# Scores of two B steps on four row groups, V products of A and C two steps together, and key and value up-projections moved into the first steps

## The chip, the cores and the metric

The kernel runs on one core of a Trainium2 chip. The core has five engines that work side by side, each through its own list of instructions in order: PE (TensorE, matrix products, with the loading of its stationary operand shown apart as PEld), DVE (VectorE), ACT (ScalarE), POOL (GpSimd) and SP (SyncE, which here only starts transfers). They meet at semaphores. The metric is the time of the program on the device in microseconds (us), the median of several executions.

## The reference

```python
# D_MODEL 1024, SEQ 512, DEPTH 2; each layer mixes four groups of 256 columns, then projects out
A = _mla(cq, ckv, krope, ...)          # q, k_nope and v come from small up-projections w_uq, w_ukv
B = _diff_attn(q, k, v, ...)           # 4 heads x 2 maps of depth 32; softmax of each, then a1 - lam * a2
C = _dsa(q, k, v, qidx, kidx, ...)     # attention over the topk keys that an index picks
D = _short_conv(b, c, h, conv_w)
# in _diff_attn, for blocks of 128 queries:
logits = jnp.einsum('bqhmd,bkhmd->bhmqk', qb, k) * scale + bias
p = _masked_softmax(logits, _chunk_mask(qpos, kpos))     # chunks of 64: causal by blocks
a = p[:, :, 0] - lam * p[:, :, 1]
return jnp.einsum('bhqk,bkhd->bqhd', a, v)
```

The rest of the model (the output projection, the feed-forward parts and a second mixing and cross attention) is computed by code that the change doesn't touch.

## The kernel before

**Large products.** Weights come through SP's queue into a ring of slots in SBUF (`load`, L699, 512 KB each). A product in full precision is made of three in a rounded format: both operands are split into a high and a low part (`whi` by ACT at L1763, `wlo` by POOL at L777 or DVE), and `products` (L1031) runs high·high, low·high and high·low for each of eight chunks of 128 rows, 512 columns wide, into one of two banks `proj`. BQ, BK, VT, GT, UQ and the like name such jobs: queries and keys of B, the values (VT), the gates (GT).

**The attention stage of a layer** is a loop of 34 steps that is written out on PE; steps 0 to 15 are B's, 16 to 23 A's and 24 to 31 C's. A step of B computes the scores of two maps of one head for one block of 128 queries: the block's number `qb` goes 0, 3, 1, 2, two steps each, and `qb` sets the width, (qb+1)·128 keys. On PE a step s is: the scores of s into the banks `score[0]` and `score[1]` (L1294 for B: depth 32, three passes, two row groups of the array side by side; L1303 for A), the V products of step s-3 (`pv`, L1344), the transposes of step s-2 (`turn`, L1320, into the banks `turned[0]` and `turned[1]` by turns), and then a number of pieces of filler: the chunks of the large products of this layer that are still to be done. `fill_plan` spreads the pieces of `FILLERS` over the steps by costs written as constants (`attention_cost`).

**What the other engines do in a step.** DVE takes the row minima of the two score banks (`row_min`, L2303), which frees the banks; ACT takes the exponentials (L1789); DVE scales and, for B, subtracts the second map (`row_scales`, L2485, L2487, L2489, whose inputs lie in SBUF); PE transposes; ACT copies the turned block to SBUF (L1969, `pT`); PE multiplies by V into `opsum[0]` or `opsum[1]` (`o` in the profile). PE's scores of step s wait until the minima of step s-1 are done (semaphore `min_ready`, 2s), its transposes wait for the scales. DVE also empties the product banks (L2314), applies gates (L2514) and does one half step of the top-k search for C in most steps (L2397, L2399). After a job is done, ACT makes the next `whi` for its slot, then POOL its `wlo`.

**The up-projections of A.** UK0, UK1 (keys, L1222) and UV0, UV1 (values, L1230) are small products of the compressed keys with weights of a slot of their own. They use one bank, `opsum[1]`, one after the other in steps 3 to 6; each waits until ACT has copied the one before out of it (L1924 and L1925 for keys, L1930 for values). VN0 to VN3 (L1137) turn a quarter of V; ACT copies it (L1909).

**Before and during this stage** the index of C is computed with products of depth 32 on four row groups (L1181), four banks at once. `TAKE` is the order in which the slots are loaded; `PREP` says after which job ACT and POOL split which slot.

Of the kernel before, what the change touches and what calls it, by code (L numbers as in the profile page):

```python
# [24 lines left out]
P = 128  # L25
# [50 lines left out]
TAKE = ("QI0", "QI1", "KR", "KI", "CQ0", "CQ1", "CKV", "BQ0", "BK0", "VT0", "BQ1", "BK1", "VT1", "UK", "UV", "UQ",  # L76
        "GT0", "GT1", "GT2", "GT3", "DB0", "VT2", "DB1", "VT3", "SQ0", "SK0", "SQ1", "SK1", "DC0", "DC1",
        "GT4", "GT5", "DH0", "DH1", "GT6", "GT7") + tuple(f"OUT{c}" for c in range(KC))
FILLERS = ("BQ1", "VN0", "BK1", "VT1", "UK0", "UQ0", "UK1", "UQ1", "UQ2", "UV0", "UQ3", "UV1", "GT0", "VN1", "GT1", "GT2", "GT3",
           "DB0", "VT2", "DB1", "VN2", "VT3", "SQ0", "SK0", "VN3", "SQ1", "SK1", "SS0", "DC0", "SR0", "DC1", "SR1",  # L80
# [10 lines left out]
SLOT_JOB = [JOB[{"UQ": "UQ3", "UK": "UQ1", "UV": "UQ3", "KI": "KR"}.get(name, name)] for name in TAKE]  # L91
# [103 lines left out]
for _n in range(2, LAYER_SLOTS + 2):  # L195
    if is_split(_n):
        PREP.setdefault({RAW[-1] + 1: "UK1", RAW[-1] + 2: "UQ2"}.get(_n, JOBS[SLOT_JOB[half_before(_n)]]), []).append(_n)

# [36 lines left out]

def attention_cost(s):

    blocks = 0.0
    if s < STEPS:
        blocks += (0.25 if s < B_STEPS or s >= C_STEP else 0.44) * (step_qb(s) + 1)  # L240
    if 2 <= s:
        blocks += (0.25 if s - 2 < B_STEPS else 0.46) * (step_qb(s - 2) + 1)
    return blocks


def fill_plan():

    pieces = []
    for name in FILLERS:
        if name in SLOT_OF:  # L250
            pieces += [(name, k, 0.68) for k in range(KC)]
        else:
            pieces.append((name, 0, {"UQ": 2.9, "UK": 1.5, "UV": 1.5, "VN": 0.5, "SS": 1.0, "SR": 1.0}[name[:2]]))
# [18 lines left out]
O_STEP = (10, 18, 22, 26, 32, 34)  # L272
SQUARE_STEP = O_STEP[1] + 1
# [118 lines left out]
def build(nc, x, wstream, params, gains, tab1, tab2, hot1, hot2, rope, ident_in, mem, lines1, lines2, out):  # L392
    ctx = ExitStack()
    with ctx:
# [173 lines left out]
        V_BANK = (opsum[1], opsum[1], opsum[0], opsum[1])  # L568
# [98 lines left out]
        def _(sp):  # L667
# [34 lines left out]
            for L in range(DEPTH):  # L702
                for i in range(LAYER_SLOTS):
                    sp.wait_ge(job_done, layer_job(L, JOBS[SLOT_JOB[i]]) + 1)
                    if i == SLOT_OF["UV"]:
                        sp.wait_ge(up_done, L * 4 + 4)
# [270 lines left out]
        def _(pe):  # L977
# [113 lines left out]
            for L in range(DEPTH):  # L1091
# [37 lines left out]
                def turn_v(n):  # L1129

                    wait_out(pe, L, f"VT{n}")
                    if n == 1:
                        pe.wait_ge(up_out, L * 4 + 4)
                    if n >= 2:
                        pe.wait_ge(o_free[n - 2], L * 3 + 1)
                    for t in range(NT):
                        mm = pe.transpose(V_BANK[n][:, t * P:(t + 1) * P], vstage[:, n % 2, t * P:(t + 1) * P], ident[:, :])  # L1137
                    mm.then_inc(v_turned, 1)
# [75 lines left out]
                def up_k(pair):  # L1214

                    w, b = raw_slot("UK"), opsum[1]
                    if pair == 0:
                        pe.wait_ge(latent_ready, L * 3 + 3)
                        pe.wait_ge(v_copied, L * 4 + 1)
                    else:  # L1220
                        pe.wait_ge(up_out, L * 4 + 1)
                    pe.matmul(b[:, :], w[:, pair * P:(pair + 1) * P], ckvn, start=True, stop=True).then_inc(up_done, 1)  # L1222

                def up_v(half):

                    w, b = raw_slot("UV"), opsum[1]
                    pe.wait_ge(up_out, L * 4 + 2 + half)
# [44 lines left out]
                def scores(s):  # L1272

                    if s == 0:
# [12 lines left out]
                    if s == C_STEP + 4:  # L1287
                        pe.wait_ge(c_ready, L * 4 + 4)
                    def parts(b, q_part, k_part, first, last):
# [20 lines left out]
                def turn(s):  # L1310

                    qb = step_qb(s)
                    if s == 0:
                        pe.wait_ge(latent_ready, L * 3 + 3)
                    pe.wait_ge(scaled_ready, L * LAYER_SM + (2 * s + 2))
                    for n, g in enumerate(step_groups(s)):
                        if g >= 2:
                            pe.wait_ge(turn_out, L * LAYER_GR + (g - 1))
                        for kb in range(qb + 1):
                            mm = pe.transpose(turned[g % 2][:, kb * P:(kb + 1) * P],  # L1320
# [3 lines left out]
                def pv(s):  # L1324
# [6 lines left out]
                    if g % 8 == 1:  # L1331
                        if o >= 2:
                            pe.wait_ge(o_free[o % 2], L * 3 + (o // 2))
                        if branch == "A":
                            pe.wait_ge(up_out, L * 4 + 4)
# [403 lines left out]
        def _(act):  # L1739
# [81 lines left out]
            for L in range(DEPTH):  # L1821
# [99 lines left out]
                def copy_up_k(pair):  # L1921

                    act.wait_ge(up_done, L * 4 + (pair + 1))
                    act.activation(kA[0:HD, 2 * pair, :], opsum[1][0:HD, :], ACT.Copy)  # L1924
                    act.activation(kA[0:HD, 2 * pair + 1, :], opsum[1][HD:P, :], ACT.Copy).then_inc(up_out, 1)  # L1925

                def copy_up_v(half):

                    act.wait_ge(up_done, L * 4 + (half + 3))
                    act.activation(vA[:, 2 * half:2 * half + 2, :], opsum[1][:, :].rearrange("p (t c) -> p t c", c=256), ACT.Copy)\  # L1930
# [31 lines left out]
                for s in range(LAST_STEP):  # L1962
                    if 2 <= s < FILL_STEPS:
                        for g in step_groups(s - 2):
# [4 lines left out]
                            act.activation(pT[:, g % 4, 0:W], turned[g % 2][:, 0:W], ACT.Copy).then_inc(turn_out, 1)  # L1969
# [12 lines left out]
                    if s < FILL_STEPS:  # L1982
                        for name in sorted(ENDED[s], key=lambda name: name[:2] != "UV"):
# [5 lines left out]
                            elif kind == "UK":  # L1989
                                copy_up_k(int(name[2]))  # L1990
                            elif kind == "UV":
                                copy_up_v(int(name[2]))
# [233 lines left out]
        def _(dve):  # L2226
# [111 lines left out]
            for L in range(DEPTH):  # L2338
# [129 lines left out]
                def row_mins(s):  # L2468
# [6 lines left out]
                    for b in range(2):  # L2475
                        row_min((2 * s + b) % 4, width(step_qb(s)), score[b], bias_of(2 * s + b))
# [98 lines left out]
                for s in range(LAST_STEP + 1):  # L2575
# [9 lines left out]
                    gates = [int(name[2]) for name in ENDED[s - 2] if name[:2] == "GT"] if 2 <= s < FILL_STEPS + 2 else []  # L2585
                    if s < MASK_STEP and len(TOPK_AT[s]) > 1:
# [8 lines left out]
                    if s in O_STEP:  # L2595
# [458 lines left out]
```

## Time and profile before

| what | value |
|---|---|
| median of 3 runs | 1780.67 us (1780.3 to 1782.26) |
| the profiled execution | 1782.3 us, of which the span from first to last instruction is 1780.5 us |
| busy PE, DVE, ACT, POOL | 99%, 60%, 42%, 23% of the span |
| granted TensorE clock, mean | 0.999 |
| attention loop, first layer | steps 0 to 15 begin at 74.18 us, steps 16 to 31 at 163.76 us |
| attention loop, second layer | step 0 begins at 382.58 us |

A matmul's busy time overlaps that of the next, since the array is a pipeline; what a product costs PE is the distance from its start to the start of the next. A busy share near 100% says that PE seldom waits, not that the array is full.

### The profile page before, as it was taken

The numbers are of one execution on the slowest core, as the hardware profiler recorded it, in microseconds if no ns is written. First come the engines' busy times: TensorE is split into PE (matmuls) and PEld (weight loads), VectorE is DVE, ScalarE is ACT, GpSimd is POOL, SyncE is SP. The second block draws the span as 40 slices with busy tenths as digits, with TensorE's granted clock in tenths as the row PEclk, the third lists the DMA queues.
The fourth block names the chain that finished last, engine by engine and source line by source line (L and its number), as shares of the span: only waits on it lengthen the run. The fifth ranks groups of instructions, "written<-read, shape, count | busy, mean of one in ns | idle before, by whom it ended". The sixth has DMA issues, their size and how long they took to land.

```text
span 1780.5 us, 25163 instructions
## 1 busy us (share of the span) xinstructions
PE 1769.6 (99%) x9274; PEld 1436.7 (81%) x9274; DVE 1065.6 (60%) x2106; ACT 748.7 (42%) x1386; POOL 408.1 (23%) x248
## 2 busy tenths in 40 slices
PE   9999999999999999999999999999999999999998
PEld 7767778776777888888888887889888888888887
DVE  5888776598877765554433546455756644555333
ACT  6464644446454533322222455555444322332222
POOL 4544543455354310000000232220200200000000
PEclk9999999999999999999999999999999999999999
DMA  5422213322212343333333522323321333333332
GB/s 189 125 79 71 60 60 87 101 76 83 70 50 60 96 137 94 99 101 94 95 106 106 160 60 84 96 72 107 95 81 51 95 95 94 94 98 102 97 105 94
DMA packets 49765, 165.53 MB, mean 93 GB/s; under 512 B 5640, under 2 KB 6152, under 8 KB 49672
## 3 DMA queue, kind: packets, MB, share of 16 engines
q1 hardware_dynamic: 48376, 161.47, 29.9%
q10 hardware_dynamic: 1296, 2.84, 0.4%
q8 instruction: 56, 0.92, 0.2%
q14 instruction: 37, 0.30, 0.1%
HBM read 162.12 MB, written 2.17 MB: 92 GB/s over the span
## 4 chain that ended last, share of the span: by engine, by line
PE 96%; DVE 2%; ACT 1%; issue 0%; DMA 0%; ACTq 0%; POOL 0%; DVEq 0%
PE proj L1031 78%; PE turned L1320 2%; PE o L1344 2%; PE score L1294 2%; PE proj L1471 1%; PE o L1579 1%; PE proj L1478 1%; PE score L1303 1%; PE o L1679 1%; PE turned L997 1%; PE turned L1558 1%; PE score L1668 1%; PE turned L1541 1%; PE score L1181 0%; PE score L1541 0%
## 5 line engine op out<-in xcount | busy, mean ns | idle before, releaser
L1031 PE MATMUL proj<-hhi,whi 128*128 128x512 f32 x1456 | 580.3, 399 | 0.0
L1031 PE MATMUL proj<-hhi,wlo 128*128 128x512 f32 x1456 | 568.0, 390 | 0.0
L1031 PE MATMUL proj<-hlo,whi 128*128 128x512 f32 x1456 | 567.4, 390 | 0.0
L1763 ACT ACTIVATE whi<-ring 128x1024 fp32r<-128x1024 f32 x279 | 295.2, 1058 | 607.0 <-PE proj L1031 593.7
L2230 DVE TENSOR_TENSOR wlo<-ring,whi 128x1024 fp32r<-128x1024 f32 x199 | 243.1, 1221 | 161.4 <-ACT whi L1763 161.0
L1031 PEld LDWEIGHTS proj<-hhi,whi 128*128 128x128 f32 x1456 | 274.3, 188 | 61.9 <-issue 9.2
L1031 PEld LDWEIGHTS proj<-hhi,wlo 128*128 128x128 f32 x1456 | 273.4, 188 | 58.7
L1031 PEld LDWEIGHTS proj<-hlo,whi 128*128 128x128 f32 x1456 | 274.0, 188 | 52.9
L777 POOL TENSOR_TENSOR wlo<-ring,whi 128x1024 fp32r<-128x1024 f32 x80 | 194.9, 2437 | 374.6 <-ACT whi L1763 374.1
L789 POOL TENSOR_TENSOR prob<-prob 128x512 f32<-128x512 f32 x36 | 56.6, 1573 | 873.9 <-ACT prob L1759 873.9
L1789 ACT ACTIVATE prob<-prob,negmax 128x256 f32<-128x256 f32 (+3 forms) x208 | 114.2, 551 | 92.8 <-DVE negmax L2303 92.1
L1031 PE MATMUL proj<-inner_hi,whi 128*128 128x512 f32 x352 | 136.9, 389 | 0.0
L1031 PE MATMUL proj<-inner_lo,whi 128*128 128x512 f32 x352 | 136.9, 389 | 0.0
L1031 PE MATMUL proj<-inner_hi,wlo 128*128 128x512 f32 x352 | 136.9, 389 | 0.0
L2303 DVE CUSTOM_DVE_ANT_0 prob<-score,arena 128x256 f32<-128x256 f32 (+3 forms) x176 | 73.9, 456 | 74.4 <-PE score L1541 62.9
L2314 DVE TENSOR_TENSOR tmp<-proj,R 128x512 f32<-128x512 f32 x48 | 33.2, 691 | 121.1 <-PE proj L1031 118.8
L1031 PE MATMUL proj<-yhi,whi 128*128 128x512 f32 x245 | 96.7, 395 | 0.1
L1031 PE MATMUL proj<-yhi,wlo 128*128 128x512 f32 x245 | 95.7, 390 | 0.0
L1031 PE MATMUL proj<-ylo,whi 128*128 128x512 f32 x245 | 95.2, 389 | 0.0
L2657 DVE TENSOR_TENSOR tmp<-tmp,proj 128x512 f32<-128x512 f32 x44 | 30.3, 689 | 103.8 <-PE proj L1031 103.5
L1969 ACT ACTIVATE pT<-turned 128x128 f32<-128x128 f32 (+3 forms) x96 | 38.5, 434 | 102.8 <-PE turned L1320 102.2
L1031 PEld LDWEIGHTS proj<-inner_lo,whi 128*128 128x128 f32 x352 | 66.1, 188 | 13.8
(346 smaller groups left out, 2443.7 us busy)
## 6 DMA issues: line engine op xcount, KB each, us to landing
ring<-wstream SPq DMA_DIRECT2D x287, 512.0 KB, 3.5
arena<-lines SPq DMA_DIRECT2D x28, 256.0 KB, 5.7
arena<-x ACTq DMA_DIRECT2D x4, 512.0 KB, 5.5
out<-arena SPq DMA_DIRECT2D x8, 256.0 KB, 2.8
arena<-mem SPq DMA_DIRECT2D x1, 1024.0 KB, 8.4
ring<-wstream ACTq DMA_DIRECT2D x2, 256.0 KB, 6.7
arena<-hot SPq DMA_DIRECT2D x2, 80.0 KB
par<-params ACTq DMA_DIRECT2D x2, 74.0 KB, 1.8
```

Source lines behind the costliest of these rows:

```text
L777: return pool.tensor_tensor(rounded(wlo[:, s, :]), ring[:, s, :], whi[:, h, :], ALU.subtract)
L789: pool.tensor_tensor(sq[:, 3, :], sq[:, 0, :] if c == 1 else sq[:, 3, :], sq_last if c == KC - 1 else sq[:, c % 3, :], ALU.add).then_inc(s ...
L1031: mm = pe.matmul(b, rounded(w), rounded(rhs(v, k)), start=(first and n == 0 and p == 0), stop=(last and n == len(blocks) - 1 and p == 2))
L1294: mm = pe.matmul(score[b][:, 0:W], rounded(q_part[rows, pair, q]), rounded(k_part[rows, pair, 0:W]), start=first, stop=last)
L1320: mm = pe.transpose(turned[g % 2][:, kb * P:(kb + 1) * P], prob[:, (2 * s + n) % 4, kb * P:(kb + 1) * P], ident[:, :])
L1344: mm = pe.matmul(opsum[o % 2][h * HD:(h + 1) * HD, qb * P:(qb + 1) * P], v, pT[:, (g - 1 + h) % 4, kb * P:(kb + 1) * P], start=(kb == 0), ...
L1763: act.activation(rounded(dst), src, ACT.Copy, scale=scale).then_inc(ready, 1)
L1789: act.activation(prob[:, i, 0:W], prob[:, i, 0:W], ACT.Exp, bias=negmax[:, i:i + 1], scale=-1.0, accum_out=rowsum[:, i:i + 1] if total is ...
L1969: act.activation(pT[:, g % 4, 0:W], turned[g % 2][:, 0:W], ACT.Copy).then_inc(turn_out, 1)
L2230: dve.tensor_tensor(rounded(wlo[:, s, :]), ring[:, s, :], whi[:, h, :], ALU.subtract).then_inc(lo_ready, 1)
L2303: dve.tensor_tensor_reduce(prob[:, i, 0:W], src[:, 0:W], bias, 1.0, 3e38, ALU.add, ALU.min, negmax[:, i:i + 1]).then_inc(min_ready, 1)
L2314: return dve.tensor_tensor(dst, src, factors, ALU.mult)
```

## The change

1. **B's scores** (`quad_step`): at even steps 2 to 14 PE issues the scores of steps s and s+1 together, as four products on the four 32-row groups into four banks: `score[0]`, `score[1]`, `turned[1]` and an `opsum` bank that is free (bank 1, from step 12 on bank 0). Odd steps 3 to 15 issue no scores. All transposes of B now go to `turned[0]`, so each waits for the copy of the one before. DVE reads the minima of odd steps from the other two banks.
2. **V products of A and C**: at even steps from 20 on PE issues `pv(s-4)` and `pv(s-3)` together; odd steps have none.
3. **UK0, UK1, UV0, UV1** are issued in step 1 into four empty banks. The first quad (step 2) waits until ACT has copied all four (`up_out`), and ACT copies them ahead of the exponentials of step 1. The slots of UK and UV are loaded ahead of that of VT1, and the splitting of VT1 and of two gate slots moves with them.
4. **The fill plan**: new costs and a new order of `FILLERS`. VN0 moves from step 1 to 2, VN1 to step 8, into `turned[0]`, so that `turn(7)` in step 9 waits for ACT's copy of VN1; VN2 and VN3 come in steps 17 and 18. In steps 0 to 7 there are 35 chunks of large products instead of 31, in steps 8 to 15 54 instead of 52, later 95 instead of 101. GT0, for example, is now done in step 5 (step 8 before), GT1 in step 8 (step 9 before).

```diff
-TAKE = (..., "BQ0", "BK0", "VT0", "BQ1", "BK1", "VT1", "UK", "UV", "UQ",
+TAKE = (..., "BQ0", "BK0", "VT0", "BQ1", "BK1", "UK", "UV", "VT1", "UQ",
-FILLERS = ("BQ1", "VN0", "BK1", "VT1", "UK0", "UQ0", "UK1", "UQ1", "UQ2", "UV0", "UQ3", "UV1", "GT0", "VN1", "GT1", "GT2", "GT3",
-           "DB0", "VT2", "DB1", "VN2", "VT3", "SQ0", "SK0", "VN3", "SQ1", "SK1", "SS0", "DC0", "SR0", "DC1", "SR1",
+FILLERS = ("BQ1", "UK0", "UK1", "UV0", "UV1", "BK1", "VN0", "VT1", "UQ0", "UQ1", "GT0", "UQ2", "UQ3", "GT1", "VN1", "GT2", "GT3",
+           "DB0", "VT2", "DB1", "VT3", "SQ0", "VN2", "SK0", "VN3", "SQ1", "SK1", "SS0", "DC0", "SR0", "DC1", "SR1",
...
+def quad_step(s):
+    return 2 <= s < B_STEPS and s % 2 == 0
...
     if s < STEPS:
-        blocks += (0.25 if s < B_STEPS or s >= C_STEP else 0.44) * (step_qb(s) + 1)
+    if quad_step(s):
+        blocks += 0.2 + 0.2 * (step_qb(s) + 1)
+    elif s < 2 or B_STEPS <= s < STEPS:
+        blocks += (0.25 if s < B_STEPS or s >= C_STEP else 0.44) * (step_qb(s) + 1)
...
-        V_BANK = (opsum[1], opsum[1], opsum[0], opsum[1])
+        V_BANK = (opsum[0], turned[0], opsum[0], opsum[1])
+        UP_BANK = {"UK0": turned[0], "UK1": turned[1], "UV0": opsum[1], "UV1": opsum[0]}
+        def turn_bank(g):
+            return turned[0] if g < B_STEPS else turned[g % 2]
+        def quad_bank(s, u):
+            return (score[0], score[1], turned[1], opsum[quad_out(s)])[u]
+        def score_bank(s, b):
+            return quad_bank(s - 1, 2 + b) if 2 <= s < B_STEPS and s % 2 else score[b]
...
                 def scores(s):
+                    if 2 <= s < B_STEPS and s % 2:
+                        return
...
+                    if quad_step(s):
+                        if s == 2:
+                            pe.wait_ge(up_out, L * 4 + 4)
...
+                        for p, (q_part, k_part) in enumerate(((bq_hi, bk_hi), (bq_hi, bk_lo), (bq_lo, bk_hi))):
+                            for u in range(4):
+                                branch, pair, qb, h, m = UNITS[2 * s + u]
+                                W, r = width(qb), HD * h + 32 * m
+                                mm = pe.matmul(quad_bank(s, u)[:, 0:W], rounded(q_part[r:r + 32, pair, qb * P:(qb + 1) * P]),
+                                               rounded(k_part[r:r + 32, pair, 0:W]), start=(p == 0), stop=(p == 2))
...
                 def turn(s):
-                    if s == 0:
-                        pe.wait_ge(latent_ready, L * 3 + 3)
+                    if s == END["VN1"] - 1:
+                        pe.wait_ge(v_copied, L * 4 + 2)
                     pe.wait_ge(scaled_ready, L * LAYER_SM + (2 * s + 2))
                     for n, g in enumerate(step_groups(s)):
-                        if g >= 2:
-                            pe.wait_ge(turn_out, L * LAYER_GR + (g - 1))
+                        if g >= 1:
+                            pe.wait_ge(turn_out, L * LAYER_GR + (g if g <= B_STEPS else g - 1))
...
-                    if s >= 3:
+                    if s % 2 == 0 and s >= B_STEPS + 4:
+                        pv(s - 4)
+                    if s % 2 == 0 and s >= 4:
                         pv(s - 3)
...
+                    for name in ENDED[s] if s < FILL_STEPS else ():      # ACT, ahead of the exponentials of step s
+                        if name[:2] == "UK":
+                            copy_up_k(int(name[2]))
+                        elif name[:2] == "UV":
+                            copy_up_v(int(name[2]))
```

PE's list before, around the scores of step 1: the two maps' products of three passes, then the transposes of a quarter of V (VN0), then BK1's chunks. `bk_hi` and `bk_lo` are the parts of B's keys, `bq_hi` and `bq_lo` those of its queries.

```order
L1294 MATMUL score0<-bk_hi_58,bq_lo_59 128x128
L1294 MATMUL score1<-bk_hi_58,bq_lo_59 128x128
L1137 MATMUL o1<-ident,arena 128x128 x4
L1031 MATMUL proj0<-hhi,whi 128x512
L1031 MATMUL proj0<-hlo,whi 128x512
```

PE's list after, at the same place:

```order
L1341 MATMUL score0<-bk_hi_58,bq_lo_59 128x128
L1341 MATMUL score1<-bk_hi_58,bq_lo_59 128x128
L1253 MATMUL turned0<-arena,ring 128x512
L1253 MATMUL turned1<-arena,ring 128x512
L1260 MATMUL o1<-ring,arena 128x256 x2
L1260 MATMUL o0<-ring,arena 128x256 x2
L1062 MATMUL proj0<-hhi,whi 128x512
```

The four up-projections stand where VN0 stood; five chunks of BK1 follow them. Then comes step 2, on PE after the change:

```order
L1330 MATMUL score0<-bk_hi_58,bq_hi_57 128x512
L1330 MATMUL score1<-bk_hi_58,bq_hi_57 128x512
L1330 MATMUL turned1<-bk_hi_58,bq_hi_57 128x512
L1330 MATMUL o1<-bk_hi_58,bq_hi_57 128x512
L1330 MATMUL score0<-bk_lo_60,bq_hi_57 128x512
L1330 MATMUL score1<-bk_lo_60,bq_hi_57 128x512
L1330 MATMUL turned1<-bk_lo_60,bq_hi_57 128x512
L1330 MATMUL o1<-bk_lo_60,bq_hi_57 128x512
...
L1367 MATMUL turned0<-ident,prob 128x128
```

The banks turned1 and o1 hold the scores of step 3. ACT's list after, at the end of step 0 and in step 1 (before the change the exponentials of step 1 followed `bq_hi` directly, and the copies came in steps 3 to 6):

```order
L1810 ACTIVATE whi<-ring 128x1024
L1810 ACTIVATE bq_hi_57<-arena 128x512
L1971 ACTIVATE arena<-turned0 64x512
L1972 ACTIVATE arena<-turned0 64x512
L1971 ACTIVATE arena<-turned1 64x512
L1972 ACTIVATE arena<-turned1 64x512
L1977 ACTIVATE arena<-o1 128x512
L1977 ACTIVATE arena<-o0 128x512
L1836 ACTIVATE prob,arena<-prob,negmax 128x128
L1836 ACTIVATE prob,rowsum<-prob,negmax 128x128
```

The first of these rows is the high part of VT1's slot. Last, PE after the change at the end of step 8 and in step 9, which has no scores now: VN1's transposes into turned0, one chunk of GT2, then `turn(7)` into the same bank.

```order
L1172 MATMUL turned0<-ident,arena 128x128 x4
L1062 MATMUL proj0<-hhi,whi 128x512
L1062 MATMUL proj0<-hlo,whi 128x512
L1062 MATMUL proj0<-hhi,wlo_49 128x512
L1367 MATMUL turned0<-ident,prob 128x128 x3
```

Between the two uses of the bank lies ACT's copy of VN1.

## Rows read from the trace of the kernel before

**Rows 1.** The page: busy times, and the chain that ended last.
```profile
PE 1769.6 (99%) x9274; PEld 1436.7 (81%) x9274; DVE 1065.6 (60%) x2106; ACT 748.7 (42%) x1386; POOL 408.1 (23%) x248
PE 96%; DVE 2%; ACT 1%; issue 0%; DMA 0%; ACTq 0%; POOL 0%; DVEq 0%
```

**Rows 2.** Windows: us, busy PE, PEld, DVE, ACT, POOL; steps 4-7, 8-15.
```profile
97.23:115.80 18.57, 18.46 (x101) 11.75 (x101) 16.71 (x66) 15.39 (x35) 8.44 (x5) 1.00 0.28 92
115.80:163.76 47.96, 47.96 (x274) 37.11 (x273) 43.37 (x132) 22.97 (x53) 28.18 (x17) 1.00 0.25 74
```

**Rows 3.** PE's timeline (start us, us, operation) around B's scores, three widths.
```profile
80.34 0.33 PE L1294 MATMUL score<-bk_hi,bq_hi 32*128 32x128 f32 x2
80.82 0.66 PE L1137 MATMUL o<-ident,arena 128*128 128x128 f32 x4
...
86.33 0.39 PE L1031 MATMUL proj<-hlo,whi 128*128 128x512 f32 x1
86.55 0.39 PE L1031 MATMUL proj<-hhi,wlo 128*128 128x512 f32 x1
86.87 0.49 PE L1294 MATMUL score<-bk_hi,bq_hi 32*128 32x512 f32 x2
...
87.76 0.33 PE L1320 MATMUL turned<-ident,prob 128*128 128x128 f32 x1
...
101.31 0.38 PE L1294 MATMUL score<-bk_hi,bq_hi 32*128 32x256 f32 x2
...
101.86 0.55 PE L1320 MATMUL turned<-ident,prob 128*128 128x128 f32 x3
```

**Rows 4.** PE's timeline around a quad of the index.
```profile
45.90 0.49 PE L1181 MATMUL score<-idx_hi 32*128 32x512 f32 x2
45.91 0.50 PE L1181 MATMUL o<-idx_hi 32*128 32x384 f32 x2
...
46.80 0.50 PE L1031 MATMUL proj<-hhi,whi 128*128 128x512 f32 x1
```

**Rows 5.** PE's timeline around V products, 4 and 16 instructions.
```profile
183.80 0.44 PE L1344 MATMUL o<-pT,arena 128*64 128x128 f32 x4
184.17 0.33 PE L1320 MATMUL turned<-ident,prob 128*128 128x128 f32 x1
...
188.17 1.09 PE L1344 MATMUL o<-pT,arena 128*64 128x128 f32 x16
189.19 0.44 PE L1320 MATMUL turned<-ident,prob 128*128 128x128 f32 x2
```

**Rows 6.** SP's issue of a slot's load; page, loads with median us to landing.
```profile
80.44 0.33 SPq L699 DMA_DIRECT2D ring<-wstream  x1
...
ring<-wstream SPq DMA_DIRECT2D x287, 512.0 KB, 3.5
```

**Rows 7.** PE's timeline: a key up-projection before (start to next).
```profile
94.56 1.02 PE L1222 MATMUL o<-arena,ring 128*128 128x512 f32 x2
95.42 1.88 PE L1211 MATMUL proj<-arena,ring 128*128 128x512 f32 x4
```

**Rows 8.** ACT's groups, steps 0-15: count | busy, mean ns | idle before.
```profile
L1763 ACT ACTIVATE whi<-ring 128x1024 fp32r<-128x1024 f32 x11 | 11.6, 1051 | 4.6 <-PE proj L1031 4.6
L1909 ACT ACTIVATE arena<-o 128x512 f32<-128x512 f32 x3 | 1.7, 574 | 0.0
L1925 ACT ACTIVATE arena<-o 64x512 f32<-64x512 f32 x2 | 1.2, 594 | 0.0
```

**Rows 9.** DVE's and POOL's timelines: scaling beside a low part, and clear of one.
```profile
134.04 2.49 POOL L777 TENSOR_TENSOR wlo<-ring,whi 128x1024 fp32r<-128x1024 f32 x1 [1.25 <-ACT whi L1763]
...
135.45 1.64 DVE L2489 SCALAR_TENSOR_TENSOR prob<-prob,rrow 128x512 f32<-128x512 f32 x1
...
99.78 0.75 DVE L2489 SCALAR_TENSOR_TENSOR prob<-prob,rrow 128x512 f32<-128x512 f32 x1
```

**Rows 10.** DVE's group, steps 4 to 15: scaling, four widths.
```profile
L2489 DVE SCALAR_TENSOR_TENSOR prob<-prob,rrow 128x256 f32<-128x256 f32 (+3 forms) x12 | 12.4, 1031 | 1.3
```

More of the change, by code:

```diff
@@ L90 @@
 SLOT_OF = {name: i for i, name in enumerate(TAKE)}
-SLOT_JOB = [JOB[{"UQ": "UQ3", "UK": "UQ1", "UV": "UQ3", "KI": "KR"}.get(name, name)] for name in TAKE]
+SLOT_JOB = [JOB[{"UQ": "UQ3", "UK": "BK1", "UV": "BK1", "KI": "KR"}.get(name, name)] for name in TAKE]
 RAW = tuple(SLOT_OF[name] for name in ("KI", "UK", "UV", "UQ"))
@@ L196 @@
     if is_split(_n):
-        PREP.setdefault({RAW[-1] + 1: "UK1", RAW[-1] + 2: "UQ2"}.get(_n, JOBS[SLOT_JOB[half_before(_n)]]), []).append(_n)
+        PREP.setdefault({RAW[-1] + 1: "VT1", RAW[-1] + 2: "UQ1"}.get(_n, JOBS[SLOT_JOB[half_before(_n)]]), []).append(_n)
 MIX_PREP = {MIX_TAKE[half_before(n) - PAIR_AT]: n for n in range(MIX_SLOT["VT0"], FFN2_AT) if is_pair(n) or is_kv(n)}
@@ L272, with quad_out @@
 O_STEP = (10, 18, 22, 26, 32, 34)
+def quad_out(s):
+    return 1 if s < B_STEPS - 4 else 0
+assert END["UV1"] < 2 and END["VN0"] < 4 < END["VN1"] < B_STEPS and END["VN2"] >= B_STEPS - 1
+assert quad_out(O_STEP[0] - 1) == 1 and quad_out(O_STEP[0] + 2) == 0
 SQUARE_STEP = O_STEP[1] + 1
@@ L1131, in turn_v @@
                     wait_out(pe, L, f"VT{n}")
+                    if n == 0:
+                        pe.wait_ge(up_out, L * 4 + 4)
                     if n == 1:
-                        pe.wait_ge(up_out, L * 4 + 4)
+                        pe.wait_ge(turn_out, L * LAYER_GR + (END["VN1"] - 1))
                     if n >= 2:
                         pe.wait_ge(o_free[n - 2], L * 3 + 1)
+                    if n == 2:
+                        pe.wait_ge(min_ready, L * LAYER_SM + 2 * B_STEPS)
                     for t in range(NT):
@@ L1350, in _ @@
                         scores(s)
-                    if s >= 3:
+                    if s % 2 == 0 and s >= B_STEPS + 4:
+                        pv(s - 4)
+                    if s % 2 == 0 and s >= 4:
                         pv(s - 3)
@@ L1968, in _ @@
                                 act.wait_ge(pv_done, L * LAYER_GR + (g - 3))
[L1969 removed]
+                            act.activation(pT[:, g % 4, 0:W], turn_bank(g)[:, 0:W], ACT.Copy).then_inc(turn_out, 1)
+                    for name in ENDED[s] if s < FILL_STEPS else ():
[3 more added lines that the diff above has]
+                            copy_up_v(int(name[2]))
                     if s < STEPS:
@@ L1982, in _ @@
                     if s < FILL_STEPS:
-                        for name in sorted(ENDED[s], key=lambda name: name[:2] != "UV"):
+                        for name in ENDED[s]:
                             kind = name[:2]
@@ L2475, in row_mins @@
                     for b in range(2):
-                        row_min((2 * s + b) % 4, width(step_qb(s)), score[b], bias_of(2 * s + b))
+                        row_min((2 * s + b) % 4, width(step_qb(s)), score_bank(s, b), bias_of(2 * s + b))
                 def row_scales(s):
@@ L2594, in _ @@
                         mask()
-                    if s in O_STEP:
+                    if s in O_STEP and s != O_STEP[1]:
                         o_out(O_STEP.index(s))
```

43 lines of the change are left out of this document (21 added, 22 removed).

## The prediction

> **What bounds the kernel now.** I read the page first. PE is busy 99% of the span and the chain that ended last runs through PE for 96% of it, with 2% on DVE and 1% on ACT [rows 1]; so time is won where PE issues less, and lost where PE must newly wait. The granted clock is 1.00 in both windows of the loop that I read [rows 2], so PE's prices below hold as they stand. The same windows show who comes second. In steps 4 to 7 DVE works 16.71 of 18.57 us, in steps 8 to 15 43.37 of 47.96 [rows 2]: DVE is 90% full just where the change shortens PE's steps. DVE's total of 60% [rows 1] hides that, since it is an average over stages with other limits.
>
> The prices come from PE's timeline, each as the distance from the first start of a phase to the start of what follows.
>
> **Odd steps of B without scores.** A step's six matmuls, two row groups by three passes, take 86.87 to 87.76 = 0.89 us at width 512, 101.31 to 101.86 = 0.55 at 256, 80.34 to 80.82 = 0.48 at 128 [rows 3]; for 384 I take the middle of the two wider ones, 0.72. Behind a product the first score starts 0.32 after the last chunk's matmul (86.55 to 86.87), where chunks follow each other by 0.22 (86.33 to 86.55) [rows 3]: 0.09 for going over. Seven odd steps (3 to 15) go: two each of 512, 256 and 384 and one of 128, so 2 x 0.89 + 2 x 0.55 + 2 x 0.72 + 0.48 = 4.80, and 7 x 0.09 = 0.63, together 5.43 us a layer. This holds if a quad takes no longer than one step's scores do now. The nearest row is the index, also of depth 32 on four row groups: its twelve matmuls run from 45.90 to 46.80, 0.90 us [rows 4], beside 0.89 for six at that width. Quads in which all four are narrow do not occur in the trace. Their price lies between one step's scores (0.48 at 128) and two (0.96); I take the first, because it is the row of the same matmuls and the index shows four groups at the price of two.
>
> The Trainium skill, page "TensorE: Matmul & The Clock Gate", section "Measured speedup vs the span model", gives four row tiles of depth 32 at 512 columns as 3.07 times faster than one after another, not 4 times. By it a quad would cost 4/3.07 = 1.3 of a step's scores, an estimate that takes 1.4 us a layer from the gain; the index row of 0.90 beside 0.89 doesn't agree with it.
>
> **V products two steps together.** Four instructions take 183.80 to 184.17 = 0.37, sixteen 188.17 to 189.19 = 1.02 [rows 5]. So one costs (1.02 - 0.37)/12 = 0.054 and a phase 0.37 - 4 x 0.054 = 0.15 by itself. Eight phases a layer go: 1.2 us. The V products now come up to a step later; before, each transposed block already lay in SBUF by then, and the wait on `pT` only gets easier.
>
> **Gross: 6.65 us a layer, 13.3 for both.** The chunks and up-projections moved by the plan are as many as before and cost the same wherever they stand: nothing.
>
> **New wait 1: the first quad waits for four copies.** PE starts step 1 at 80.34, takes 0.48 for scores [rows 3], four up-projections of 0.86 each (94.56 to 95.42; the value ones have half the width and twice the number) [rows 7] and five chunks of 0.68 (three matmuls of 0.22 to 0.23 [rows 3]): it is ready for the quad at about 87.8 to 88.0. ACT has, ahead of the copies, the high part of VT1. By the new order of `TAKE`, VT1's load is the one that SP issues at 80.44, when BQ1 is done; it lands 3.5 later [rows 6], at about 84.0; the high part takes 1.05, `bq_hi` of half its width about 0.6, then four key copies of 0.59 and two value copies of about the same, 3.5 together [rows 8]: 84.0 + 1.05 + 0.6 + 3.5 = 89.1. PE waits about 1.1; nothing covers it, since PE's list stands still behind the quad. In the second layer the same sum gives 1.3. I take 1.2. It would be zero with VT1's load earlier, up to 2.5 if the load is late by another 1.3. The exponentials of step 1 stand behind these copies and come 4 us later (84.8 to about 89), but their transposes are due only in step 3, behind the seven pieces of filler of step 2.
>
> **New wait 2: the quad of step 8 waits for DVE.** From GT0's end (now in step 5) PE has in steps 6 and 7: the quad 0.72, V products and two transposes about 1.3, UQ2 and UQ3 at 1.88 [rows 7], three chunks 2.04, in all 7.8 us. DVE's work in two steps, at the mean of steps 4 to 7, is 2 x 16.71/4 = 8.4 [rows 2], and GT0's eviction (a pass over 512 columns, about 0.7 by the clear scaling [rows 9]) is new in it, of which some half overlaps what lies before: 8.6. PE waits 0.75 if scaling runs clear. If it falls behind a low part on POOL it takes far longer: beside POOL's 2.49 us that began at 134.04 a scaling took 1.64 instead of 0.75, and ended 0.56 after POOL [rows 9]; the twelve scalings of steps 4 to 15 average 1.03 over all widths [rows 10], above the clear one of the widest. By my count of DVE's order the scaling of step 5 comes due at about the time at which POOL begins on GT2's low part; starting right behind it costs up to 2.49 + 0.56 - 0.75 = 2.3, some 2.0 with a start a little later, and the wait becomes 2.7. That is even odds: 1.7 on average.
>
> The Trainium skill, page "SBUF — State Buffer", section "Who interferes with whom", says that a DVE instruction with two SBUF inputs contends with a GpSimd instruction that reads SBUF, and that whoever is first holds the shared pair for its whole instruction. The row of 1.64 agrees.
>
> **New wait 3: turn(7) waits for VN1's copy.** Between the two uses of `turned[0]` PE has one chunk, 0.68. The copy takes 0.57, but a high part of 1.05 can stand before it [rows 8]: from 0 to 0.95, I take 0.6, since GT3's high part comes due there.
>
> **New wait 4: steps 10 to 15.** The stretch 8 to 15 loses four odd steps' scores and entries (0.48 + 0.89 + 0.55 + 0.72 + 0.36 = 3.0) and gains two chunks (1.36): 47.96 becomes 46.3, with 43.37 of DVE work in it [rows 2]. DVE still fits, at 94%; 0 to 0.9, I take 0.2.
>
> **Sum.** Waits 1.2 + 1.7 + 0.6 + 0.2 = 3.7 a layer, 2.75 without the collision on POOL and 4.7 with it. Net 6.65 - 3.7 = 2.95 a layer, 5.9 for both. The profiled execution took 1782.3 (span 1780.5), 1.6 above the median of 1780.67; the new one should come to about 1776.4 in such a profile, and **1774.8** as a median. Its own range, from no collision in either layer to one in both: 1780.67 - 7.8 = 1772.9 to 1780.67 - 3.9 = 1776.8.
>
> **Rivals.**
> 1. No wait appears: loads land early, DVE has slack after all. Then 13.3 come back whole: 1767.4. For it: DVE has 10% idle. Against: the sum of wait 1 leaves PE 1.1 short with every duration from a row. Chance 0.12.
> 2. Quads cost more than a step's scores. If those of 128 and 256 save nothing, 0.48 + 2 x 0.55 = 1.6 a layer goes: 1778.0. For it: no narrow quad in the trace; against it the index row [rows 4]. The page's 1.3 for every width would come to about the same, 1777.7. Chance 0.10.
> 3. The other side: DVE becomes the bound of steps 4 to 15, place `min_ready` before the quads. PE meets DVE at every second step only, but there with two shortened steps behind it. If the quads of 8, 12 and 14 meet it (2.7 + 2.3 + 2.3) and waits 1 and 3 stand (1.2 + 0.7), 9.2 a layer is lost against 6.65 won: 1780.67 + 5.1 = 1785.8. It decides from 6.65 of waits a layer on. For it: DVE at 90% and scalings already lengthened [rows 2, 10]; against it: in steps 12 and 14 the low parts would all have to fall badly. Chance 0.10.
> 4. The quads do not run side by side, and a quad takes two steps' time. Then only 0.63 + 1.2 are won against 2.75 of waits: 1782.5. Against it the index row. Chance 0.05.
>
> **Numbers.** The forecast has 0.63. I call 0.2%, 3.6 us, about what a measurement of this kernel can tell from no change; it ends at 1777.1. Most of the forecast (0.54 of its 0.63) and rival 1 lie below it: faster 0.66. The rest of the forecast, rival 2 and half of rival 4 and a bit of 3: same 0.25; slower 0.09. The range holds the forecast, rivals 1 and 2 and stops at no change: 1767.3 to 1780.7.
>
> **What would show it.** PE's timeline: odd steps of B go from V products or filler to transposes with no scores; quads start four matmuls together, 0.48 to 0.9 long by width; V products of A and C in pairs. A wait of about 1 us on ACT ahead of the quad of step 2, and 0.7 to 2.7 on DVE's `negmax` ahead of that of step 8; 0.6 before `turn(7)`. Wrong would be: quads of 128 longer than 0.6, waits on DVE ahead of several quads, or other waits in A's and C's steps, where I count none.

## The result, and the profile after

The changed kernel took 1784.20 us (median of 22 runs, 1782.37 to 1785.11) beside 1781.04 for the kernel before (22 runs): a ratio of 1.0014, 95% interval 1.0009 to 1.0020. It is a little slower, by less than the 0.2% that I called no change, and far from the 1774.8 of the prediction. The profiled execution of the changed kernel took 1783.11 us with a span of 1781.3.

The page of the changed kernel, busy times and chain, as in [rows 1]:

```profile
PE 1758.0 (99%) x9274; PEld 1433.1 (80%) x9274; DVE 1079.9 (61%) x2106; ACT 749.2 (42%) x1386; POOL 408.1 (23%) x248
PE 90%; DVE 5%; issue 2%; POOL 1%; ACT 1%; DMA 1%; ACTq 0%; DVEq 0%; POOLq 0%
```

PE is busy for 11.6 us less than in [rows 1], so work did leave it. But DVE, whose list is as long as before, is busy for 14.3 us more, and 6% of the chain went from PE to others. What PE waits for (us in total, times, longest):

```profile
PE proj L1062 <- POOL wlo L808: 4.2, 4, 1.5
PE score L1330 <- ACT arena L1977: 2.8, 2, 1.6
PE proj L1062 <- ACT arena L1966: 2.5, 2, 1.3
...
PE score L1350 <- DVE negmax L2351: 1.3, 2, 0.6
PE turned L1367 <- ACT arena L1956: 1.1, 2, 0.6
PE score L1330 <- DVE negmax L2351: 0.9, 2, 0.4
```

None of these six stands in the kernel before. They make 12.8 us, close to the 13.3 that the prediction counted as gain before waits.

The quads themselves, PE's timeline (start us, us, operation), for each of the four widths the first row and what follows:

```profile
89.31 0.50 PE L1330 MATMUL score<-bk_hi,bq_hi 32*128 32x512 f32 x2 [1.27 <-ACT arena L1977]
89.32 0.49 PE L1330 MATMUL turned<-bk_hi,bq_hi 32*128 32x512 f32 x1
...
90.21 0.33 PE L1367 MATMUL turned<-ident,prob 128*128 128x128 f32 x1
...
100.32 0.38 PE L1330 MATMUL score<-bk_hi,bq_hi 32*128 32x256 f32 x2
...
100.87 0.33 PE L1389 MATMUL o<-pT,arena 128*64 128x128 f32 x2
...
109.51 0.44 PE L1330 MATMUL score<-bk_hi,bq_hi 32*128 32x384 f32 x2
...
110.24 1.09 PE L1389 MATMUL o<-pT,arena 128*64 128x128 f32 x16
...
119.70 0.33 PE L1330 MATMUL score<-bk_hi,bq_hi 32*128 32x128 f32 x2 [0.43 <-DVE negmax L2351]
...
120.19 0.33 PE L1389 MATMUL o<-pT,arena 128*64 128x128 f32 x2
```

Four row groups take 0.90 at 512 (89.31 to 90.21), 0.55 at 256 and 0.49 at 128, where two took 0.89, 0.55 and 0.48 [rows 3], and 0.73 at 384, for which the prediction took 0.72. The price is as forecast, for narrow quads too.

DVE in the same windows as [rows 2], steps 4 to 7 and 8 to 15 (us; busy us of PE, PEld, DVE, ACT, POOL):

```profile
100.32:119.70 19.38, 17.60 (x102) 11.23 (x102) 16.68 (x60) 11.82 (x26) 6.12 (x3) 1.00 0.20 71
119.70:168.80 49.10, 46.44 (x274) 36.18 (x275) 47.29 (x135) 23.22 (x57) 31.40 (x18) 1.00 0.22 66
```

And the group of B's scaling, all 32 of both layers (busy us, mean ns), of the kernel before and then of the changed one:

```profile
L2489 DVE SCALAR_TENSOR_TENSOR prob<-prob,rrow 128x128 f32<-128x128 f32 (+3 forms) x32 | 30.0, 939 | 3.3
L2537 DVE SCALAR_TENSOR_TENSOR prob<-prob,rrow 128x128 f32<-128x128 f32 (+3 forms) x32 | 43.2, 1349 | 3.3
```

Steps 8 to 15 got longer, not shorter, and DVE works 96% of them. The 32 scalings took 30.0 us before (mean 0.94) and take 43.2 now (mean 1.35), 13.2 more. That is near DVE's 14.3 only in the balance: the 64 scalings of A and C rose by 6.7 as well (45.6 to 52.3), and the gating passes fell by 5.1 (17.4 to 12.3).

How one of them stops PE can be read from the timeline of the changed kernel, steps 5 to 8 and then 11 and 12, ordered by engine (PE's rows last in each part), with the rows between them left out:

```profile
110.81 2.35 POOL L808 TENSOR_TENSOR wlo<-ring,whi 128x1024 fp32r<-128x1024 f32 x1 [2.37 <-ACT whi L1810]
109.61 0.69 DVE L2362 TENSOR_TENSOR yT<-proj,R 128x512 f32<-128x512 f32 x1 [1.80 <-PE proj L1062]
110.86 2.58 DVE L2537 SCALAR_TENSOR_TENSOR prob<-prob,rrow 128x256 f32<-128x256 f32 x1
113.37 0.55 DVE L2351 CUSTOM_DVE_ANT_0 prob<-score,arena 128x384 f32<-128x384 f32 x1
113.96 0.61 ACT L1836 ACTIVATE prob<-prob,negmax 128x384 f32<-128x384 f32 x1 [1.84 <-DVE negmax L2351]
116.28 0.59 ACT L1966 ACTIVATE arena<-proj 32x512 f32<-32x512 f32 x1
116.92 0.50 PE L1062 MATMUL proj<-hhi,whi 128*128 128x512 f32 x1 [1.27 <-ACT arena L1966]
...
142.35 0.72 ACT L1836 ACTIVATE prob<-prob,negmax 128x512 f32<-128x512 f32 x1 [3.87 <-DVE negmax L2351]
143.78 1.04 ACT L1810 ACTIVATE whi<-ring 128x1024 fp32r<-128x1024 f32 x1
144.96 2.77 POOL L808 TENSOR_TENSOR wlo<-ring,whi 128x1024 fp32r<-128x1024 f32 x1 [0.75 <-ACT whi L1810]
145.96 0.40 PE L1062 MATMUL proj<-hhi,wlo 128*128 128x512 f32 x1
147.88 0.47 PE L1062 MATMUL proj<-hhi,whi 128*128 128x512 f32 x1 [1.52 <-POOL wlo L808]
148.19 0.39 PE L1062 MATMUL proj<-hlo,whi 128*128 128x512 f32 x1
```

GT0 ends at 109.6. ACT makes the next high part and POOL starts on its low part at 110.81. DVE evicts GT0 and starts the scaling of step 5 at 110.86, 0.05 behind POOL: it takes 2.58, where one of the same width took 0.49 at 105.14 with POOL idle. The minima of step 6 come 2 us late, so do the exponentials, and behind these on ACT stand UQ2's copies, whose bank PE wants for GT1: 1.27 of idle, called a wait on ACT by the profile. In the second part DVE is so late that ACT has idled 3.87 us before the exponentials of step 11; the high part for VT2, free to go when GT3 ended at 139.4, stands behind them, POOL starts late, and PE waits 1.52, called a wait on POOL. By these rows both begin at DVE; whether they go away with the collisions is what the experiments ask.

**TensorE's clock, and why the medians differ by more than the profiles.** The spans differ by 0.8 us, the medians by 3.2. Windows of PE (us, busy, granted clock) in the second layer, of the kernel before and then of the changed one:

```profile
512.00:516.00 4.00, 4.00 (x27) 1.00 0.26 78
516.00:520.00 4.00, 4.00 (x18) 0.59 0.15 57
```

```profile
512.00:516.00 4.00, 4.00 (x41) 1.00 0.45 131
516.00:520.00 4.00, 3.35 (x15) 0.79 0.01 4
520.00:524.00 4.00, 4.00 (x17) 0.78 0.00 0
```

In step 23, right behind sixteen matmuls of two columns each (`SS0`, 1.7 us), the clock is partly at the lower of its levels, 1.2 GHz, and that costs about 4 x 0.41 = 1.6 and 4 x (0.21 + 0.22) = 1.7 us, an estimate from these windows. In the first layer of either profile it stays at 1.00. So both profiles hold one such fall, and the other 2.4 us between the medians lie in executions without a profile. Of these the record has only the mean clock, to a thousandth, which is 1.8 us of a run. Within one kernel the time follows it: the runs of `act_early` below go from 1780.56 us at 1.0 to 1787.49 at 0.996. Between the two kernels it is too coarse: the profiles hold the same fall and have means of 0.999 and 0.998, since the end of the span counts too, where PE has no work (0.73 from 1776 to 1780 in the changed kernel). That the changed kernel, which idles another 0.65 us right behind `SS0`, has one fall more in most executions fits the size, but is not shown.

### The profile page after: what moved, and what is told of

The parts are those of the page before. It is cut to its first block, busy times and chain, and to the rows that moved or that the text cites. A ratio compares the mean times of both kernels' runs of the same rounds, so it can differ in the third digit from the quotient of the medians.

```text
span 1781.3 us, 25161 instructions
## 1 busy us (share of the span) xinstructions
PE 1758.0 (99%) x9274; PEld 1433.1 (80%) x9274; DVE 1079.9 (61%) x2106; ACT 749.2 (42%) x1386; POOL 408.1 (23%) x248
## 4 chain that ended last, share of the span: by engine, by line
PE 90%; DVE 5%; issue 2%; POOL 1%; ACT 1%; DMA 1%; ACTq 0%; DVEq 0%; POOLq 0%
PE proj L1062 74%; PE turned L1367 1%; PE proj L1518 1%; PE o L1389 1%; PE o L1626 1%; PE proj L1525 1%; DVE arena L2447 1%; PE o L1726 1%; PE score L1350 1%; PE turned L1028 1%; PE turned L1605 1%; PE score L1341 1%; PE score L1715 1%; POOL wlo L808 1%; DVE arena L2445 1%
## 5 line engine op out<-in xcount | busy, mean ns | idle before, releaser
L2351 DVE CUSTOM_DVE_ANT_0 prob<-score,arena 128x256 f32<-128x256 f32 (+3 forms) x148 | 60.5, 444 | 74.4 <-PE score L1588 62.9
L1062 PEld LDWEIGHTS proj<-inner_hi,whi 128*128 128x128 f32 x352 | 66.1, 188 | 13.8
```

Of the source, the lines that this page charges most:

```text
L1062: mm = pe.matmul(b, rounded(w), rounded(rhs(v, k)), start=(first and n == 0 and p == 0), stop=(last and n == len(blocks) - 1 and p == 2))
L2351: dve.tensor_tensor_reduce(prob[:, i, 0:W], src[:, 0:W], bias, 1.0, 3e38, ALU.add, ALU.min, negmax[:, i:i + 1]).then_inc(min_ready, 1)
```

## Experiments

Theory one: DVE's scalings run beside POOL's parts, take up to 2.6 us, and all the late waits follow. Theory two, the rival: the new order of fillers and copies makes the waits, and DVE has too little time anyway since PE's steps are shorter. Ratios are to the kernel before, in the same session. The changed kernel was timed only in the session of the result; the kernel before took 1781.04 us there and 1781.21 to 1781.42 in the others, so differences to the changed kernel are good to some 0.4 us.

The medians also hold the falls of the clock. Where that matters, a line shows the first layer alone, from the first score of step 0 to that of the second layer: us, busy PE (matmuls), granted clock, which is 1.00 in each that is shown (the last two numbers are the DMA's). What the busy time leaves of the length is PE's idle time. The kernel before and the changed one:

```profile
74.18:382.58 308.40, 308.22 (x1700) 1.00 0.25 76
74.27:382.77 308.50, 302.10 (x1699) 1.00 0.25 76
```

So the change took 6.1 us of work out of the layer and put 6.2 us of idle time into it (6.40 where 0.18 was).

**pv_pairs**: the V products alone, in the kernel before.

```diff
-                    if s >= 3:
+                    if 3 <= s < B_STEPS + 3:
                         pv(s - 3)
+                    if s % 2 == 0 and s >= B_STEPS + 4:
+                        pv(s - 4)
+                        pv(s - 3)
```

> The kernel before with only the V products of A and C taken two steps together at even steps from 20 on; everything else as before. By the prediction's price, eight phases a layer at 0.15 us each go: 2.4 us faster than before, about 1778.6, and no new wait. Rival: the pairs make blocks of turned scores wait longer, or the phases cost nothing by themselves: no change, 1781.

1778.87 beside 1781.39, ratio 0.9985 (0.9976 to 0.9994): 2.5 us, as priced. The first layer says the same without the clock's part:

```profile
74.85:382.01 307.16, 306.44 (x1699) 1.00 0.26 76
```

It is 1.24 shorter, twice that for both layers. But new waits on DVE in C's steps, which I had not expected (1.2 us in all), are in the number. PE's work fell by 1.78 a layer (308.22 to 306.44), for 1.2 priced: the pairs are worth more than their price, and half a microsecond a layer was lost again.

**step1_fill**: more work ahead of the first quad.

```diff
 PLAN = fill_plan()
+PLAN[1] += PLAN[2][:3]
+del PLAN[2][:3]
```

> The changed kernel with the last three chunks of BK1 in step 1 instead of step 2, so that PE has 2 us more work ahead of the first quad's wait for the four copies. If that wait is a loss by itself: 1.3 us and 1.6 us come back, about 1781.4. Rival (DVE sets the pace of steps 5 to 13, so PE only comes earlier to the next wait): the wait of step 2 goes, those of steps 7, 8, 12 grow by as much, 1784.

1780.97, ratio 0.9997 (0.9988 to 1.0006), 3.2 below the changed kernel's 1784.20, for 1781.4 expected. The wait on the four copies (2.8) is gone, waits of 0.2 and 0.25 on an eviction came in step 4, and those of steps 7, 8, 12, 13 and 23 are as they were. So wait 1 was a loss by itself; the rival, that it would come back later, is out.

**pool_hold**: POOL keeps off the scaling.

```diff
                 for s in range(FILL_STEPS):
+                    if 4 <= s < C_STEP and any(PREP.get(name) for name in ENDED[s]):
+                        pool.wait_ge(scaled_ready, L * LAYER_SM + (2 * s + 2))
                     for name in ENDED[s]:
                         prepare_after(name)
...
-                    if 0 <= s - ROPE_STEP < 4:
-                        q_rope(s - ROPE_STEP, ...)
+                    for part in ROPE_AT.get(s, ()):
+                        if 4 <= s < B_STEPS:
+                            pool.wait_ge(scaled_ready, L * LAYER_SM + (2 * s + 2))
+                        q_rope(part // 3, part % 3, ...)
```

> The changed kernel, in which POOL begins the low part of a job ended in steps 4 to 23 only when DVE's scaling of that step is done, and spreads the rotary products of the queries (twelve operations) over eleven steps instead of four. No computation is left out. Theory one (DVE's scaling runs beside POOL and takes up to 2.6 us instead of 0.75, and that makes the later waits): mean scaling time of B falls to below 0.75 us, PE's waits in steps 7, 8, 12, 13 and 23 (4.5 us a layer in the changed kernel) go almost whole, time 1784.2 - 8 = about 1776. Theory two (the waits come from the new order of the fillers and from copies that stand behind exponentials, and DVE is short of time anyway as PE's steps are shorter): the scaling gets shorter but the waits stay, within 2 us of 1784.

1784.60, ratio 1.0017 (1.0008 to 1.0027): no gain, and by the time alone theory one would be dead. The group of the scalings, what PE waits for, and two windows of PE in the second layer (us, busy, granted clock) say otherwise:

```profile
L2549 DVE SCALAR_TENSOR_TENSOR prob<-prob,rrow 128x128 f32<-128x128 f32 (+3 forms) x32 | 18.7, 585 | 3.3
```

```profile
PE score L1362 <- POOL arena L902: 5.0, 2, 2.5
PE score L1342 <- ACT arena L1989: 3.0, 2, 1.6
PE proj L1072 <- POOL wlo L809: 2.7, 4, 1.0
```

```profile
504.00:508.00 4.00, 2.79 (x20) 0.60 0.02 4
508.00:512.00 4.00, 4.00 (x19) 0.55 0.00 0
```

The scalings fell from 43.2 to 18.7 us, the waits behind UQ's copies and A's wait in step 23 are gone. But my spreading left the rotary products of A's last heads, for which PE now waits in step 20, so late that PE waited 2.5 us for them in each layer, and behind that wait the clock was at 0.60 and 0.55 for 8 us in the second layer and at 0.77 and 0.80 for 8 us in the first. The experiment made its own loss.

**before_hold**: the hold and spreading of pool_hold in the kernel before.

> The kernel before with the same hold on POOL as in the run on the changed kernel, nothing else. Theory one: DVE's scalings get shorter by some 5 us in all, but PE hardly waits for DVE in the kernel before, so the time stays within 1 us of 1781. Rival: the hold is worth as much here as in the changed kernel (it helps whatever the change does), then 1776 or less; or POOL's parts come late now and PE waits for them: above 1782.

1783.76, ratio 1.0013 (1.0004 to 1.0022), 2.4 slower, where theory one had expected no change within 1 us. The scalings fell from 30.0 to 19.6 us and it gained nothing; new waits of PE on minima (0.9) and on low parts (0.5) are part of the 2.4, the rest is not traced. So the rival of a gain here is out, and the case that POOL's parts come late has come in part. Scaling time is worth something only where PE waits for DVE.

**pool_hold2**: the hold with the rotary products done by step 15.

```diff
+ROPE_AT = {8: (0,), 9: (1,), 10: (2, 3, 4), 11: (5,), 12: (6, 7), 13: (8,), 14: (9, 10), 15: (11,)}
```

> As the run pool_hold, but the twelve rotary products on POOL are done by step 15, so that A's scores don't wait 2.5 us for them in step 20 of each layer. Theory one (scaling beside POOL causes the waits of steps 7, 12, 13 and 23): those waits total under 1.5 us a layer instead of 4.0, no wait on POOL's rotary product, no fall of the granted clock in steps 20 to 23, time about 1784.2 - 5 - 2 = 1777. Theory two (the late waits on low parts come from ACT's high parts that stand behind exponentials): 1.3 us a layer stay in steps 12 and 13, time about 1780.

1775.98, ratio 0.9973 (0.9963 to 0.9983): 8.2 below the changed kernel, for 1777 expected. What PE waits for, and the first layer:

```profile
PE proj L1072 <- POOL wlo L809: 3.3, 2, 1.7
PE score L1342 <- ACT arena L1989: 3.1, 2, 1.9
...
PE turned L1379 <- ACT arena L1968: 1.1, 2, 0.6
PE score L1342 <- DVE negmax L2363: 0.9, 2, 0.4
```

```profile
74.54:379.94 305.40, 301.42 (x1700) 1.00 0.25 77
```

The waits behind UQ's copies, in step 13 and in step 23 are gone, as theory one has it. That of step 12 stayed, 1.66, more than the 1.5 that theory one had left for all of them: there ACT's high part behind the exponentials and now the hold itself make POOL late, so theory two has a share of that one. The 0.43 before the quad of step 8 stayed too. The first layer is 3.1 shorter than in the changed kernel, 2.4 of it idle time; this profile has no fall of the clock where that of the changed kernel had one of 1.7, and twice 3.1 with 1.7 makes most of the 8.2. The 32 scalings take 18.7 us as in pool_hold, 0.59 each. The Trainium skill, page "SBUF — State Buffer", section "Who interferes with whom", says that a DVE instruction with two SBUF inputs contends with a GpSimd instruction that reads SBUF, and calls the pair of ports that they share an exclusive lock. The 2.58 us beside POOL's 2.35, and 0.59 on average with POOL held, agree.

**act_early**: theory two's own mend alone.

```diff
+                    first = [name for name in EARLY[s] if name[:2] in ("GT", "DB")] if s < B_STEPS else []
+                    for name in first:
+                        prepare_after(name)
                     if s < STEPS:
                         for a in (2 * s, 2 * s + 1):
                             softmax_exp(...)
```

> The changed kernel, in which ACT makes the high part that follows GT3 (step 11) and DB0 (step 12) ahead of that step's exponentials instead of behind them. Theory two: the waits for low parts in steps 12 and 13 (1.5 and 0.6 us a layer) go, about 1784.2 - 4 = 1780. Theory one: POOL's part then only starts earlier, beside another scaling, and DVE's lateness shows elsewhere: 1783 to 1784.

1783.60, ratio 1.0012 (1.0003 to 1.0021). The wait of step 12 fell from 1.5 to 0.5, that of step 13 rose from 0.6 to 1.0, the others stayed; the first layer is 0.6 shorter than in the changed kernel (307.89 for 308.50). As theory one expected, with a small gain for theory two.

**quads_from_8**: scores of steps 2 to 7 as before the change.

```diff
+QUAD_FROM = 8
...
-                    if 2 <= s < B_STEPS and s % 2:
+                    if QUAD_FROM <= s < B_STEPS and s % 2:
                         return
```

> The changed kernel with the scores of steps 2 to 7 issued step by step as before the change; quads only from step 8 on; fill plan and all else as changed. If the quads of steps 2 to 6 are worth their matmuls (0.89 + 0.55 + 0.72 and 0.27 for going over a layer): 4.9 us slower than the changed kernel, 1789. If DVE sets the pace up to step 8: the waits of steps 7 and 8 (1.7 us a layer) shrink in exchange, and it costs 1.5 us in all or less, 1785.5.

1786.64, ratio 1.0027 (1.0017 to 1.0038): 2.4 slower than the changed kernel, between the two. The first layer:

```profile
74.58:384.55 309.97, 304.24 (x1701) 1.00 0.25 76
```

PE works 2.1 us more than in the changed kernel (304.24 for 302.10), for 2.43 priced, and idles 0.7 less: the waits of steps 7 and 8 went from 1.7 to 1.3, that of step 2 from 1.3 to 1.0. So under a third of the quads' work had been paid back in waits. The layer is 1.5 longer, 2.9 for both; that the medians show 2.4 may be the clock, which does not fall in this profile. The 32 scalings take 43.2 us here too: without the quads of steps 2 to 6 the collisions cost DVE as much, so it is not these quads that make them. The new plan with no quads at all was not run.

**all_mended**: hold, rotary products by step 15, early high parts and step1_fill together, VN1 three chunks earlier, and the double half steps of the top-k search mostly in odd steps. In a step whose job ends early POOL is held only until the scaling of the step before.

```diff
+PLAN[8].remove(("VN1", 0))
+PLAN[8].insert(3, ("VN1", 0))
+PLAN[1] += PLAN[2][:3]
+del PLAN[2][:3]
...
+ENDED[8].sort(key=lambda name: name != "VN1")
...
+TOPK_TWO = (0, 3, 7, 9, 13, 15, 19)
```

> The changed kernel with five mends together: three chunks more ahead of the first quad (step1_fill), POOL's hold and rotary products by step 15 (pool_hold2), the early high parts (act_early), VN1's transposes three chunks earlier and its copy ahead of the next high part, and a second half step of the top-k search in odd steps instead of even ones. If the price of the quads and of the pairs was right and only the waits were missed, nearly all of the measured gross gain of 12 us appears: 1770 to 1772. If DVE or ACT is simply too full for the shorter steps, other waits take their place: 1776 or more.

1768.39 (1768.11 to 1769.04), ratio 0.9924 (0.9911 to 0.9938): 13 us faster than the kernel before, and below the 1770 to 1772 expected. PE idles 1.2 us in both layers together. The first layer:

```profile
74.85:376.88 302.03, 301.50 (x1700) 1.00 0.26 78
```

It is 6.4 shorter than in the kernel before, with 0.35 of new idle time in it, so PE's work fell by 6.7, for 6.65 forecast.

**mended_no_hold**: the same without the hold.

> As all_mended, but POOL as in the changed kernel (no hold, the rotary products in four steps). If the collisions of POOL with DVE's scaling are the main cause, the scalings go back to about 43 us in all, waits of 3 us a layer or more return in steps 7 to 23, and the time is about 1776. If moving the other work was what mattered, it stays below 1771.

1780.12, ratio 0.9992 (0.9983 to 1.0001), 4 more than expected. The scalings and the first layer:

```profile
L2550 DVE SCALAR_TENSOR_TENSOR prob<-prob,rrow 128x128 f32<-128x128 f32 (+3 forms) x32 | 36.9, 1154 | 3.7 <-DVE rrow L2548 0.5
```

```profile
74.81:380.98 306.17, 301.98 (x1700) 1.00 0.25 77
```

The scalings are at 36.9 us, where all_mended has 22.0; PE waits 3.8 on low parts, 2.5 behind UQ's copies and 1.3 in step 23. The first layer is 4.1 longer than in all_mended, 8.3 for both; the rest of the 11.7 between the medians is in part the clock, which falls in this profile and not in that of all_mended. With every other mend in place the collisions alone cost most of the gain. The hold and the spreading of the rotary products, which both keep POOL off the scalings, were not run apart.

**mended_quads_8**: all_mended with quads from step 8 on.

> As all_mended, with quads only from step 8 on. Here PE waits for little, so the quads of steps 2 to 6 should show their full price: 0.89 + 0.55 + 0.72 + 3 x 0.09 = 2.43 us a layer, 4.9 in all, about 1773.3. If DVE still sets the pace there, less than half of it: below 1771.

1772.29, ratio 0.9950 (0.9937 to 0.9964): 3.9 more than all_mended, with 0.7 less of waits, so 4.6 for 4.9 expected.

```profile
74.13:377.97 303.84, 303.62 (x1699) 1.00 0.26 77
```

In the first layer PE works 2.1 us more than in all_mended (303.62 for 301.50), as in quads_from_8, for 2.43. The quads of steps 2 to 6 are worth nearly their price where nothing waits.

## Why the prediction was wrong

**Right, and shown.** The gross gain: 6.65 a layer (its terms, 5.43 and 1.2, add to 6.63), and PE's work fell by 6.7 in all_mended. A quad takes what one step's scores took, at every width, and rival 2 is out. The total is luck in part, though: the pairs took 1.8 out of a layer, for 1.2, and the quads of steps 2 to 6 2.1, for 2.43. The factor of 1.3 that I estimated from the Trainium skill's page "TensorE: Matmul & The Clock Gate", section "Measured speedup vs the span model", is seen at no width here (0.90 beside 0.89, 0.49 beside 0.48); the page compares four tiles with one after another, while a step's scores already ran on two row groups. Wait 1: forecast 1.2 a layer, measured 1.27 and 1.57, by the chain of copies that I had summed. Wait 3: 0.6, measured 0.55.

**Right by luck.** Wait 2: 1.7, measured 1.27 + 0.43 in steps 7 and 8. My 1.7 was the mean of 0.75 and 2.7; the collision came, for which I had 2.7, and cost less. Its path was another, too: 1.27 ran through ACT's exponentials and UQ2's bank, and the 0.43 before the quad stayed when POOL was held.

**Wrong: "New wait 4: steps 10 to 15".** I put 43.37 us of DVE work into a shorter stretch, found 94% and took 0.2 a layer. DVE's work there became 47.29. Measured were waits of 1.52 + 0.59 = 2.1 in steps 12 and 13, and 0.65 in step 23, in A's steps, "where I count none". Against the forecast of 7.4 us of waits for both layers stand 12.8; of the 5.4 between, 3.8 is this wait, 1.3 that of step 23, 0.4 wait 1. The failing assumption is that DVE's work is a constant which is moved. The scalings' length depends on where POOL stands, and a change of the plan moves POOL's parts. The waits of steps 7, 13 and 23 go when POOL is held (pool_hold2) and come back without the hold (mended_no_hold). That of step 12 has two causes: 1.66 with the hold alone, 0.5 with the early high part alone (and 1.0 in step 13), none that shows with both. I had the row (1.64 beside POOL) and the group that showed it as common [rows 9, 10], used it at one step, and left it out of the sum over the others.

Rival 3 named this mechanism and got 0.10, since I took it for several mishaps. But where DVE waits for the job that ends a step, its eviction (0.7) and two small operations (0.55) put the scaling just behind POOL's start, which itself follows ACT's high part of 1.05: 0.05 behind in step 5, 0.14 in step 9. In steps 11 and 12 it starts 1.1 behind. Rival 3 also had the wrong place: only 0.9 of the 12.8 us stand on DVE's minima before a quad, the rest on copies, on low parts and in step 23.

**Not counted.** A wait costs more than its row. The row counts from the end of PE's last matmul, but without a wait the next one starts before that end. In step 12 the last matmul starts at 145.96 and the next at 147.88, 1.92 later where chunks follow each other by 0.23: 1.69 lost for 1.52 in the row. And the matmul behind it starts 0.31 later (148.19) instead of 0.23. In the first layer PE is busy for 302.10 us in the changed kernel, with seven waits, and for 301.50 in all_mended, with one: some 0.6 a layer, an estimate.

So for the profile, forecast at 1776.4: + 5.4 (waits) + 1.2 (what the waits cost beside their rows) = 1783.0, for 1783.11. For the median the same sum gives 1774.8 + 6.6 = 1781.4, for 1784.20. The 2.8 between stay open; more falls of the clock in executions without a profile would fit.

## What to carry to other kernels

Where an engine is 90% full and its instructions lengthen beside another's, don't carry its busy time over to the new order as a constant: list each instruction that can be lengthened, with what will run beside it at its new place. A saving on the engine that sets the time is worth its matmuls only where the next engine has room, so mend the second engine first, and read a mend by its waits as well as by its time: pool_hold gained nothing and was right.

## What the runs showed that I had not expected

Holding POOL back by one wait each, with the rotary products spread, was worth 8.2 us in the changed kernel and 11.7 beside the other mends (6.2 and 8.3 by the first layers, where the clock has no part), and nothing before the change. And TensorE's granted clock fell in the second layer of both kernels behind sixteen two-column matmuls in which PE counts as busy throughout (0.59; 0.79 and 0.78), though not in the first; it fell behind 2.5 us of plain waiting in both layers of pool_hold, while it stayed at 1.00 behind waits of 1.27 to 1.92 (1.92 before the first quad of pool_hold2's second layer).
